# Head of the two mixture-of-experts stages: order of GpSimd's power, router-bias wait, position matmuls, and when the first weight slots are reloaded

## Chip, cores and metric

One core of one Trainium2 chip runs the whole program. The metric is device time of one execution in microseconds (us), and the figure compared is the median of the runs.

## What is computed

Two transformer blocks run one after the other on 256 tokens of width 1024, all in float32. Each is a mixer followed by a mixture of 32 experts (4 groups of 8). Only the expert part is touched by the change; cut to that:

```python
g_logits = x @ w_grp + b_grp;  g_idx = argmax(g_logits)        # 4 groups
e_logits = (x @ w_exp + b_exp)[group g_idx]                    # 8 experts of it
top_v, top_i = top_k(e_logits, 2)
gate = softmax(top_v) * softmax(g_logits)[g_idx]
for e in range(32):                                            # w1, w3: 1024x512, w2: 512x1024
    out += weight_e * ((silu(x_e @ w1[e]) * (x_e @ w3[e])) @ w2[e])
h = rmsnorm(h + out)
```

An expert's three matrices are 2,048 KB each, 6.29 MB together, so the weights of 32 experts are 201 MB in each of the two expert stages.

## The kernel before

**Stages.** `mixer1`, `moe` (first experts, "stage 1"), `mixer2`, `moe` again (second experts, "stage 2"). Between stages there is a barrier of all engines. Stage 1 starts at 192.2 us of the profiled execution and stage 2 at 1215.1 us.

**Weight sets.** SBUF holds two sets of three slots (w1, w3, w2) in `weight_ring`, and in stage 2 a third set, `e_third`. Expert `i` uses set `i % SETS`; SETS is 2 in stage 1 and 3 in stage 2. Experts 0 and 1 are loaded while the mixer before still runs (in stage 1 two matrices of expert 1 are loaded at the stage's start). The other loads are issued by the SyncE queue (SP), in one written order: for expert `i` it waits until expert `i - SETS` has finished its up projection (`s_up`), issues w1 and w3 (L1253, L1254, both by the helper's line L152), waits for that expert's down projection (`s_down`), and issues w2. An instruction on SP that waits holds up all that are queued behind it. `load_last` already loads the last two experts in halves.

**Head of a stage.** SP issues the router's weights (L1242, L1243: many short pieces), the router's biases (L1244, L1245), then in stage 1 the loads of the context part, and in stage 2 four pieces of `gate_m` (L1262), `final_row` (L1267) and the third set (expert 2). GpSimd (POOL) prepares `rw` and `halves`, then five small tables (L1310 to L1314), and then computes the inverse root with an ALU power (L1317) of the row statistics that VectorE (DVE) makes (L1517). With it ACT and DVE scale the rows (L1452, L1519), TensorE (PE) transposes them (L1329) and multiplies them by the router's weights (L1337; it waits for all four router loads, `s_router` 64). DVE adds the biases (L1546 to L1550) and picks the experts in a long chain of small instructions up to `both` (L1573). Five matmuls (L1355 to L1359) give each token its position in its expert (`ps` bank 4, columns 0 to 63) and each expert's total (columns 64 to 95). From the positions DVE makes `Gt` (L1580, L1582), PE gathers the rows of expert 0 (L1363), DVE transposes them (`xT`), and expert 0's up projection (L1398) begins.

**An expert on PE.** Up projection: 8 steps of k by 4 column blocks, 64 matmul records. Then the gather of the next expert, the combine of the one before (L1371) and the down projection (L1423). Expert 0 has the residual (L1346) in place of the combine, and a transposition of table rows (L1429). In stage 1, 18 groups of a projection of the context rows (L989, L991) are interleaved with experts 1 to 27, at fixed steps.

Of the kernel before, what the change touches and what calls it, by code (L numbers as in the profile page):

```python
# [5 lines left out]
ALU = mybir.AluOpType  # L6
# [9 lines left out]
TT = T // P  # L16
KD = D // P
# [13 lines left out]
NE, NG, EPG = 32, 4, 8  # L31
# [1109 lines left out]
def moe(c, t, w, last):  # L1141

    nc, ps, h = c.nc, c.ps, c.h
    with phase(nc, w["tag"]) as (st, sb, sem):
# [65 lines left out]
        s_router, s_frow, s_gm = sem("router_in"), sem("final_row_in"), sem("gate_in")  # L1210
# [30 lines left out]
        def _(sp):  # L1241
            sp.dma_start(rw[:, :, NE:RW], t[w["ew"]][0].rearrange("(k p) e -> p k e", p=P)).then_inc(s_router, 16)  # L1242
            sp.dma_start(rw[:, :, 0:NG], t[w["gw"]][0].rearrange("(k p) e -> p k e", p=P)).then_inc(s_router, 16)  # L1243
            sp.dma_start(rb[:, 0:NG], row_view(t[w["gb"]], 0, NG)).then_inc(s_router, 16)  # L1244
            sp.dma_start(rb[:, NG:NR], row_view(t[w["eb"]], 0, NE)).then_inc(s_router, 16)  # L1245
# [3 lines left out]
            def load_expert(u, e, done):  # L1249

                if done is not None:
                    sp.wait_ge(s_up, done)
                load_one(c, sp, sems, u, 0, W, e, third)  # L1253
                load_one(c, sp, sems, u, 1, W, e, third)  # L1254
                if done is not None:
                    sp.wait_ge(s_down, done)
                load_one(c, sp, sems, u, 2, W, e, third)

            if mod is not None:
                for m in range(4):  # L1260
                    at = 5 * D + m * 256
                    sp.dma_start(gate_m[32 * m:32 * m + 32, :], row_view(mod, at, at + 256, 32)).then_inc(s_gm, 16)  # L1262
# [5 lines left out]
            for i in range(2, STATIC):  # L1268
                load_expert(i % SETS, bass.ds(i, 1), i - SETS + 1 if i >= SETS else None)
                if x is not None:  # L1270
                    x.sp_step(sp, i)
            def load_last(u, e, done):
# [33 lines left out]
        def _(pool):  # L1306
            link = lambda ins: c.pch(pool, ins)
            pool.memset(rw[:, :, NG:NE], 0.0).then_inc(s_pad, 1)  # L1308
            pool.tensor_tensor(halves, c.ident[:, 0:RW], c.ident[:, RW:P], ALU.add).then_inc(s_pad, 1)  # L1309
            link(pool.iota(ie[:], [[1, NE]], base=0, channel_multiplier=0, allow_small_or_imprecise_dtypes=True))  # L1310
# [5 lines left out]
            pool.wait_ge(s_stat, 1)  # L1316
            pool.tensor_tensor(stat[:, 1, 0:TT], stat[:, 0, 0:TT], c.neg_half[:, 0:TT], ALU.pow).then_inc(s_rstd, 1)  # L1317
# [6 lines left out]
        def _(pe):  # L1324
# [6 lines left out]
            pe.wait_ge(s_router, 64)  # L1331
# [23 lines left out]
            pe.matmul(ps[:, 4, 0:NE], tri[:], both[:, 0, :], start=True, stop=True)  # L1355
            pe.matmul(ps[:, 4, NE:2 * NE], c.ones[:], both[:, 0, :], start=True, stop=False)
            pe.matmul(ps[:, 4, NE:2 * NE], tri[:], both[:, 1, :], start=False, stop=True)
            pe.matmul(ps[:, 4, 2 * NE:3 * NE], c.ones[:], both[:, 0, :], start=True, stop=False)
            pe.matmul(ps[:, 4, 2 * NE:3 * NE], c.ones[:], both[:, 1, :], start=False, stop=True).then_inc(s_pos, 1)  # L1359
# [18 lines left out]
            def expert(i, q, u):  # L1378
# [7 lines left out]
                for k in range(KD):  # L1386
                    if known and k == 0:
                        pe.wait_ge(s_w1[u], 16 * q + 16)
                        pe.wait_ge(s_w3[u], 16 * q + 16)
                    elif not known and k % 4 == 0:  # L1390
                        if k == 0:
                            pe.wait_ge(s_w1[u], 16 * q + (16 * TURNS + 16))
                            pe.wait_ge(s_w3[u], 16 * q + (16 * TURNS + 16))
                        else:
                            pe.wait_ge(s_half[2 * u], 16 * q + 16)
                            pe.wait_ge(s_half[2 * u + 1], 16 * q + 16)
                    for j in range(4):
                        mm = pe.matmul(ps[32 * j:32 * j + 32, 4, 0:256].rearrange("p (w f) -> p w f", w=2),  # L1398
                                       xT[:, k, :], w13[:, :, k, j * P:(j + 1) * P],
                                       start=(k == 0), stop=(k == KD - 1))  # L1400
                mm.then_inc(s_up, 1)
# [111 lines left out]
        def _(dve):  # L1513
# [17 lines left out]
            dve.wait_ge(s_router, 64)  # L1531
# [52 lines left out]
            link(dve.tensor_scalar(nblk[:], ps[:, 4, 2 * NE:3 * NE], float(SLOTS - 1), float(SLOTS), ALU.add, ALU.max))  # L1584
# [1000 lines left out]
```

## Time and profile before

| | us |
|---|---|
| median of 3 runs | 1696.2 (1696.05 to 1697.95) |
| the profiled execution: its time | 1696.79 |
| the profiled execution: its span | 1695.0 |
| PE busy | 1400.5 (83%) |
| DVE busy | 647.6 (38%) |
| ACT busy | 245.8 (15%) |
| POOL busy | 58.0 (3%) |
| DMA moved | 528.51 MB, mean 312 GB/s |

The span is what the trace shows; 1.8 us of the time lie around it. Busy shares are means over stages with different limits, so each stage is read by itself, from windows and the timeline.

### The profile page before, as it was taken

To read this page: it belongs to the slowest core of one execution; us is meant where nothing else is said; L and a number is where in the kernel's file an instruction comes from. 1 tells how busy PE (TensorE), PEld (TensorE's weight loads), DVE (VectorE), ACT (ScalarE), POOL (GpSimd) and SP (SyncE) were. 2 spreads that over 40 slices of the span, in tenths; PEclk is the share of its full clock that TensorE was granted. 3 is DMA by queue.
4 is the path that set the end of the run, shared out by engine and by line. 5 is a ranking of instruction groups with operands and counts; after the bars stand their busy time and mean duration, and the time that the engine had idled before them with its cause. 6 is when DMAs were issued, how large, how long until landed. Compare 5 with 4: busy or idle time off the path is not lost. (4 is left out here: it accounts for less than half of the span.)

```text
span 1695.0 us, 27911 instructions
## 1 busy us (share of the span) xinstructions
PE 1400.5 (83%) x12075; PEld 917.9 (54%) x12075; DVE 647.6 (38%) x1786; ACT 245.8 (15%) x502; POOL 58.0 (3%) x88
## 2 busy tenths in 40 slices
PE   7999798998779888769999999998787666666664
PEld 6556455665456555448865845887344333333332
DVE  3624347322233333321487732433264223333324
ACT  2321313100011111022222212211100000000000
POOL 1300100000000000020000100000000000000000
PEclk9999989999899888979999999999888777887878
DMA  9879488999999999974433242422889999999996
GB/s 338 240 271 372 152 338 348 421 415 422 415 417 414 421 415 420 423 262 149 150 112 112 82 156 85 149 100 77 332 369 427 427 426 426 428 426 426 428 424 255
DMA packets 110090, 528.51 MB, mean 312 GB/s; under 512 B 16680, under 2 KB 35312, under 8 KB 84368
## 3 DMA queue, kind: packets, MB, share of 16 engines
q1 hardware_dynamic: 105600, 522.70, 76.9%
q0 software_dynamic: 1936, 3.92, 1.0%
q8 instruction: 96, 1.57, 0.4%
q10 hardware_dynamic: 2432, 0.10, 0.1%
q14 instruction: 26, 0.21, 0.0%
HBM read 525.64 MB, written 1.06 MB: 311 GB/s over the span
## 5 line engine op out<-in xcount | busy, mean ns | idle before, releaser
L1398 PE MATMUL ps<-weight_ring,e_xT 128*32 128x256 f32 x3456 | 257.9, 463 | 164.1 <-DMA weight_ring<-in_w_up_dram 96.2
L1398 PEld LDWEIGHTS ps<-weight_ring,e_xT 128*32 128x32 f32 x3456 | 140.6, 132 | 277.4 <-issue 233.4
L1658 DVE TENSOR_TENSOR e_g<-e_act_g,ps 128x128 f32<-128x128 f32 x64 | 24.9, 389 | 274.0 <-ACT e_act_g L1481 272.9
L1481 ACT ACTIVATE e_act_g<-ps 128x128 f32<-128x128 f32 x64 | 17.8, 278 | 626.8 <-PE ps L1398 626.8
L1423 PE MATMUL ps<-weight_ring,e_gT 128*32 128x256 f32 x1728 | 104.4, 382 | 4.8 <-DVE e_gT L1662 1.5
L1656 DVE TENSOR_TENSOR e_act_g<-e_act_g,ps 128x128 f32<-128x128 f32 x32 | 9.2, 287 | 229.6 <-ACT e_act_g L1481 229.4
L1398 PE MATMUL ps<-e_third,e_xT 128*32 128x256 f32 x640 | 55.7, 524 | 46.3 <-DMA e_third<-in_w_up_dram 46.3
L989 PE MATMUL ps<-e_nT,e_ctx_w 128*128 128x256 f32 x320 | 76.2, 399 | 4.3 <-DVE e_ctx_gcols L1090 2.3
L1423 PEld LDWEIGHTS ps<-weight_ring,e_gT 128*32 128x32 f32 x1728 | 52.1, 109 | 49.7 <-issue 20.2
L1371 PE MATMUL ps<-e_y,e_GwT 32*128 32x256 f32 x1024 | 73.7, 402 | 2.1 <-DVE e_y L1690 1.5
L1363 PE MATMUL ps<-e_n,e_Gt 128*32 128x256 f32 x1056 | 72.8, 393 | 2.0 <-DVE e_Gt L1582 1.9
L989 PEld LDWEIGHTS ps<-e_nT,e_ctx_w 128*128 128x128 f32 x320 | 63.1, 200 | 17.0 <-issue 5.0
L1398 PEld LDWEIGHTS ps<-e_third,e_xT 128*32 128x32 f32 x640 | 30.1, 149 | 71.7 <-issue 67.3
L1371 PEld LDWEIGHTS ps<-e_y,e_GwT 32*128 32x128 f32 x1024 | 46.6, 185 | 30.5 <-issue 26.0
L991 PE MATMUL ps<-e_ctx_w,e_nT 128*128 128x256 f32 x256 | 59.5, 386 | 0.0
L2045 PE MATMUL ps<-weight_ring,m_nTp 128*128 128x512 f32 x128 | 57.2, 608 | 0.0
L1963 PE MATMUL ps<-weight_ring,m_nT 128*128 128x512 f32 x128 | 56.2, 592 | 0.0
L2089 PE MATMUL ps<-m_nT,weight_ring 128*128 128x256 f32 x256 | 56.2, 379 | 0.0
L1952 PE MATMUL ps<-m_nT,weight_ring 128*128 128x256 f32 x256 | 55.4, 379 | 0.0
L991 PEld LDWEIGHTS ps<-e_ctx_w,e_nT 128*128 128x128 f32 x256 | 47.3, 190 | 11.1 <-issue 5.3
L2089 PEld LDWEIGHTS ps<-m_nT,weight_ring 128*128 128x128 f32 x256 | 48.6, 190 | 6.6
L1952 PEld LDWEIGHTS ps<-m_nT,weight_ring 128*128 128x128 f32 x256 | 48.6, 190 | 6.6
(520 smaller groups left out, 1913.0 us busy)
## 6 DMA issues: line engine op xcount, KB each, us to landing
weight_ring<-in_expert_w_dram SPq DMA_DIRECT2D x92, 2048.0 KB, 19.6
weight_ring<-in_w_in_dram SPq DMA_DIRECT2D x26, 2048.0 KB, 8.4
weight_ring<-in_w_down_dram SPq DMA_DIRECT2D x22, 2048.0 KB, 39.3
weight_ring<-in_w_gate_dram SPq DMA_DIRECT2D x20, 2048.0 KB, 33.2
weight_ring<-in_w_up_dram SPq DMA_DIRECT2D x20, 2048.0 KB, 37.8
weight_ring<-in_w_ada_dram SPq DMA_DIRECT2D x12, 2048.0 KB, 9.0
e_third<-in_w_gate_dram SPq DMA_DIRECT2D x10, 2048.0 KB, 33.2
e_third<-in_w_up_dram SPq DMA_DIRECT2D x10, 2048.0 KB, 37.7
```

What stands on the lines that cost most here:

```text
L989: mm = pe.matmul(o, w[:, k, j * P:(j + 1) * P], nT[:, k, :], start=(k == 0), stop=(k == KD - 1))
L991: mm = pe.matmul(o, nT[:, k, j * P:(j + 1) * P], w[:, k, :], start=(k == 0), stop=False)
L1363: mm = pe.matmul(ps[32 * j:32 * j + 32, 5, 0:256], Gt[:, tt, :], n[:, tt, j * 256:(j + 1) * 256], start=(tt == 0), stop=(tt == TT - 1))
L1371: mm = pe.matmul(ps[:, m, tt * 256:(tt + 1) * 256], GwT[r, tt * P:(tt + 1) * P], y[r, :], start=False, stop=False, skip_group_check=True)
L1398: mm = pe.matmul(ps[32 * j:32 * j + 32, 4, 0:256].rearrange("p (w f) -> p w f", w=2), xT[:, k, :], w13[:, :, k, j * P:(j + 1) * P], start= ...
L1423: mm = pe.matmul(ps[32 * m:32 * m + 32, 5, 0:256], gT[:, j, :], w2[:, j, m * 256:(m + 1) * 256], start=(j == 0), stop=(j == KF - 1))
L1481: act.activation(act_g[:], ps[:, 4, 0:P], gated).then_inc(s_silu, 1)
L1658: dve.tensor_tensor(g[:], spread(act_g[:]), spread(ps[:, 4, P:2 * P]), ALU.mult).then_inc(s_g, 1)
L1952: mm = pe.matmul(ps[:, 4 + j % 4, 0:T], w[:, k, (j % 4) * P:(j % 4 + 1) * P], nT[:, k, :], start=(k == 0), stop=(k == KD - 1))
L1963: mm = pe.matmul(ps[:, 6 + j % 2, :], nT[:, k, tile * P:(tile + 1) * P], w[:, k, :], start=(k == 0), stop=(k == KD - 1))
L2045: mm = pe.matmul(ps[:, j % 4, :], nTp[:, k, tile * P:(tile + 1) * P], w[:, k, :], start=(k == 0), stop=(k == KD - 1))
L2089: mm = pe.matmul(ps[:, 2 + f % 2, 0:T], w[:, k, j * P:(j + 1) * P], rhs[:, k, :], start=(k == 0), stop=(k == KD - 1))
```

## The change

- POOL's power comes directly after the two preparations; then POOL issues the two bias loads itself, on its own queue (semaphore `s_rb`); the five small tables come after them.
- PE waits for the two router weight loads only (`s_router` 32); DVE waits for the biases (`s_rb` 32) ahead of the copy at L1546.
- The positions come from two matmuls (the first now 64 columns wide); the totals follow in two more, in bank 6, with a semaphore of their own (`s_tot`).
- Set 0's first reload (expert SETS) is issued in halves: the first halves of w1 and w3 when expert 0's up projection is half done (`s_uph`), the second halves when it is done.
- In stage 2 the third set is loaded ahead of `gate_m` and `final_row`.

```diff
+            if done == 1:                                    # in load_expert
+                for half in range(2):
+                    sp.wait_ge((s_uph, s_up)[half], 1)
+                    cs = slice(half * KD * FF // 2, (half + 1) * KD * FF // 2)
+                    for which in range(2):
+                        sp.dma_start(c.ring[:, which, cs].rearrange("p (o n) -> p o n", o=1),
+                                     W[which][0, e].rearrange("o (p k) f -> p o (k f)", k=KD)[:, :, cs]).then_inc((s_first, sems)[half][which], 16)
...
-            sp.dma_start(rb[:, 0:NG], row_view(t[w["gb"]], 0, NG)).then_inc(s_router, 16)
-            sp.dma_start(rb[:, NG:NR], row_view(t[w["eb"]], 0, NE)).then_inc(s_router, 16)
...
+            for i in range(2, SETS):
+                load_expert(i, bass.ds(i, 1), None)
             if mod is not None:
                 for m in range(4):
...
-            for i in range(2, STATIC):
-                load_expert(i % SETS, bass.ds(i, 1), i - SETS + 1 if i >= SETS else None)
+            for i in range(SETS, STATIC):
+                load_expert(i % SETS, bass.ds(i, 1), i - SETS + 1)
...
             pool.tensor_tensor(halves, c.ident[:, 0:RW], c.ident[:, RW:P], ALU.add).then_inc(s_pad, 1)
+            pool.wait_ge(s_stat, 1)
+            pool.tensor_tensor(stat[:, 1, 0:TT], stat[:, 0, 0:TT], c.neg_half[:, 0:TT], ALU.pow).then_inc(s_rstd, 1)
+            pool.dma_start(rb[:, 0:NG], row_view(t[w["gb"]], 0, NG)).then_inc(s_rb, 16)
+            pool.dma_start(rb[:, NG:NR], row_view(t[w["eb"]], 0, NE)).then_inc(s_rb, 16)
...
-            pool.wait_ge(s_stat, 1)
-            pool.tensor_tensor(stat[:, 1, 0:TT], stat[:, 0, 0:TT], c.neg_half[:, 0:TT], ALU.pow).then_inc(s_rstd, 1)
...
-            pe.wait_ge(s_router, 64)
+            pe.wait_ge(s_router, 32)
...
-            pe.matmul(ps[:, 4, 0:NE], tri[:], both[:, 0, :], start=True, stop=True)
-            pe.matmul(ps[:, 4, NE:2 * NE], c.ones[:], both[:, 0, :], start=True, stop=False)
-            pe.matmul(ps[:, 4, NE:2 * NE], tri[:], both[:, 1, :], start=False, stop=True)
-            pe.matmul(ps[:, 4, 2 * NE:3 * NE], c.ones[:], both[:, 0, :], start=True, stop=False)
-            pe.matmul(ps[:, 4, 2 * NE:3 * NE], c.ones[:], both[:, 1, :], start=False, stop=True).then_inc(s_pos, 1)
+            pe.matmul(ps[:, 4, 0:2 * NE], tri[:], both[:].rearrange("p t e -> p (t e)"), start=True, stop=False, skip_group_check=True)
+            pe.matmul(ps[:, 4, NE:2 * NE], c.ones[:], both[:, 0, :], start=False, stop=True, skip_group_check=True).then_inc(s_pos, 1)
+            pe.matmul(ps[:, 6, 0:NE], c.ones[:], both[:, 0, :], start=True, stop=False, skip_group_check=True)
+            pe.matmul(ps[:, 6, 0:NE], c.ones[:], both[:, 1, :], start=False, stop=True, skip_group_check=True).then_inc(s_tot, 1)
...
+                        if i == SETS:
+                            pe.wait_ge(s_first[0], 16)
+                            pe.wait_ge(s_first[1], 16)
...
+                    if known and i == 0 and k == KD // 2 - 1:
+                        mm.then_inc(s_uph, 1)
...
-            dve.wait_ge(s_router, 64)
+            dve.wait_ge(s_rb, 32)
...
-            link(dve.tensor_scalar(nblk[:], ps[:, 4, 2 * NE:3 * NE], float(SLOTS - 1), float(SLOTS), ALU.add, ALU.max))
+            dve.wait_ge(s_tot, 1)
+            link(dve.tensor_scalar(nblk[:], ps[:, 6, 0:NE], float(SLOTS - 1), float(SLOTS), ALU.add, ALU.max))
```

## Rows read from the trace of the kernel before

**Rows 1.** The page, part 2: GB/s moved in each of 40 slices of 42.4 us.

```profile
GB/s 338 240 271 372 152 338 348 421 415 422 415 417 414 421 415 420 423 262 149 150 112 112 82 156 85 149 100 77 332 369 427 427 426 426 428 426 426 428 424 255
```

**Rows 2.** Windows in stage 1: stretch, its us, busy by engine, PEclk, DMA share, GB/s.

```profile
218.00:220.00 2.00, 2.00 (x33) 0.85 (x25) 1.74 (x10) 0.00 (x0) 0.00 (x0) 0.82 0.89 143
...
250.00:254.00 4.00, 4.00 (x25) 3.16 (x28) 0.00 (x0) 0.77 (x2) 0.00 (x0) 1.00 0.32 131
...
282.00:286.00 4.00, 4.00 (x35) 3.01 (x37) 0.23 (x1) 0.77 (x2) 0.00 (x0) 1.00 0.37 160
```

**Rows 3.** Timeline of stage 1: start us, us, engine, line, instruction, [idle before <- releaser].

```profile
193.53 0.17 DVE L1517 TENSOR_SCALAR e_stat<-e_stat 128x2 f32<-128x2 f32 x1
...
194.81 0.70 POOL L1317 TENSOR_TENSOR e_stat<-e_stat,neg_half 128x2 f32<-128x2 f32 x1
...
198.02 19.60 SPq L859 DMA_DIRECT2D e_ctx_lbl<-in_hg_lb_logits_dram  x4
...
209.88 0.39 PE L1358 MATMUL ps<-e_both,ones 128*128 128x32 f32 x2
...
210.10 0.39 PE L1359 MATMUL ps<-e_both,ones 128*128 128x32 f32 x2
...
214.05 5.93 PE L1398 MATMUL ps<-weight_ring,e_xT 128*32 128x256 f32 x64 [1.08 <-DVE e_xT L1539]
...
253.59 3.66 PE L1398 MATMUL ps<-weight_ring,e_xT 128*32 128x256 f32 x64
...
285.08 1.93 PE L1423 MATMUL ps<-weight_ring,e_gT 128*32 128x256 f32 x32
```

**Rows 4.** Windows at the head of stage 2.

```profile
1224.00:1226.00 2.00, 2.00 (x14) 1.18 (x12) 0.41 (x1) 0.88 (x1) 0.00 (x0) 0.59 0.91 266
...
1242.00:1244.00 2.00, 2.00 (x36) 1.08 (x32) 1.79 (x12) 0.00 (x0) 0.00 (x0) 0.83 0.03 8
1244.00:1246.00 2.00, 2.00 (x19) 0.83 (x12) 1.79 (x10) 0.28 (x1) 0.00 (x0) 1.00 0.48 98
1246.00:1248.00 2.00, 2.00 (x6) 0.76 (x4) 0.30 (x1) 0.00 (x0) 0.00 (x0) 1.00 0.69 246
```

**Rows 5.** Timeline at the head of stage 2.

```profile
1216.23 4.08 SPq L1244 DMA_DIRECT2D e_rb<-in_b_group_dram  x1
...
1216.46 0.17 DVE L1517 TENSOR_SCALAR e_stat<-e_stat 128x2 f32<-128x2 f32 x1
...
1217.74 0.72 POOL L1317 TENSOR_TENSOR e_stat<-e_stat,neg_half 128x2 f32<-128x2 f32 x1
...
1218.50 0.75 DVE L1519 TENSOR_SCALAR e_n<-residual,e_stat 128x1024 f32<-128x1024 f32 x1 [1.87 <-POOL e_stat L1317]
...
1223.53 2.97 PE L1337 MATMUL ps<-e_nT,e_rw 128*64 128x256 f32 x16 [0.15 <-DMA e_rb<-in_b_router_dram]
...
1226.62 0.42 DVE L1546 COPY e_sq<-ps 128x256 f32<-128x256 f32 x1 [2.21 <-PE ps L1337]
...
1234.07 0.61 PE L1358 MATMUL ps<-e_both,ones 128*128 128x32 f32 x2
...
1234.49 0.61 PE L1359 MATMUL ps<-e_both,ones 128*128 128x32 f32 x2
...
1239.53 5.20 PE L1398 MATMUL ps<-weight_ring,e_xT 128*32 128x256 f32 x64 [1.56 <-DVE e_xT L1543]
...
1244.80 0.33 SPq L152 DMA_DIRECT2D weight_ring<-in_w_gate_dram  x1
...
1257.55 0.33 SPq L152 DMA_DIRECT2D weight_ring<-in_w_gate_dram  x1
```

**Rows 6.** Timeline: one load issued by POOL.

```profile
753.08 0.95 POOL L118 DMA_DIRECT2D expert_gain<-in_norm_g_dram  x1
```

**Rows 7.** View of line L1880: POOL's 8 loads of 256 KB, issue to landing.

```profile
DMA to landing us min/median/max: 3.7/6.2/7.6
```

**Rows 8.** Window in stage 2 while 1,024 KB halves of an expert flow.

```profile
1654.00:1658.00 4.00, 2.79 (x48) 1.39 (x40) 2.12 (x7) 0.00 (x0) 0.00 (x0) 1.00 0.99 416
```

More of the change, by code:

```diff
@@ L1208, in moe @@
         x = context(c, t, sb, sem, nT, sq, wide) if "context" in w else None
-        s_router, s_frow, s_gm = sem("router_in"), sem("final_row_in"), sem("gate_in")
+        s_router, s_rb, s_frow, s_gm = sem("router_in"), sem("router_bias_in"), sem("final_row_in"), sem("gate_in")
+        s_first, s_uph, s_tot = [sem(f"first_half_in{j}") for j in range(2)], sem("half_up_done"), sem("totals_done")
         s_sq, s_stat, s_rstd, s_n = sem("squares"), sem("stat"), sem("rstd"), sem("normed")
@@ L1249, in load_expert @@
             def load_expert(u, e, done):
[L1251 to L1254, printed above, removed]
+                if done == 1:
[5 more added lines that the diff above has]
+                                         W[which][0, e].rearrange("o (p k) f -> p o (k f)", k=KD)[:, :, cs]).then_inc((s_first, sems)[half][which], 16)
+                else:
+                    if done is not None:
+                        sp.wait_ge(s_up, done)
+                    load_one(c, sp, sems, u, 0, W, e, third)
+                    load_one(c, sp, sems, u, 1, W, e, third)
                 if done is not None:
```

## The prediction

> **What bounds the kernel now.** I read the page's slices first. In both expert stages the bytes moved stand near 425 GB/s for hundreds of microseconds (from 297 us on in stage 1, from 1271 us on in stage 2) [rows 1]. An expert is 6.29 MB, so at 425 GB/s it takes 14.8 us, and a stage's length is nearly its bytes over that rate. A stage therefore gets shorter only where the DMA engines stand idle while weights remain to be loaded, or ahead of that. I looked for those holes in windows of 2 and 4 us, and in the timeline for what ends each.
>
> Stage 2 has one hole: 8 GB/s moved in 1242 to 1244 [rows 4]. The third set is in, and nothing else may be loaded until set 0 is free. SP issues expert 3 at 1244.80, when expert 0's up projection (1239.53, 5.20 us) is done [rows 5]. In 1244 to 1248 only 0.69 MB moved in place of 1.70 MB [rows 4]; the missing 1.01 MB are 2.4 us of full rate, so the flow counts as restarted at 1246.4, 1.6 us after the issue. From there it does not stop. Everything from the stage's start to 1246.4 is therefore on the path, and it is a chain of small steps on DVE, POOL and PE.
>
> Stage 1 has two later holes, 131 GB/s in 250 to 254 and 160 GB/s in 282 to 286 [rows 2]. PE sets them, not the loads: expert 2's up projection starts at 253.59 behind context work with no wait for a load, and the second hole ends after expert 3's down projection (285.08, 1.93 us), which frees its slot [rows 3]. So up to 287 us stage 1 is a chain on PE, ACT and DVE that begins with the same head as stage 2; after that it is bytes.
>
> **Power first on POOL.** It could run when POOL is done with the two preparations and DVE with L1517. The latter ends at 193.70 and 1216.63, the power starts at 194.81 and 1217.74 [rows 3, 5]. With 0.1 us for the semaphore it starts at 193.8 and 1216.7: 1.0 us off each stage's head. The tables now come behind it and behind two bias issues of about 0.95 us each [rows 6]; the tables themselves are the 1.0 us by which the power was late, so they are done near 1220.5, and DVE first reads them behind L1546 (1226.62 [rows 5]). Cost nothing; without that cover each microsecond would count in full.
>
> **Bias later, from POOL.** In stage 2 PE lost only 0.15 us to the bias before L1337 [rows 5], but with the power 1.0 us earlier the bias would have eaten that gain, so the new wait is what lets it through. DVE's new wait sits in front of the copy, 1226.62 before [rows 5] and 1225.6 after; everything DVE does up to expert 0 is queued behind it. POOL issues the second bias load near 1218.4; with 3.7 to 7.6 us to landing [rows 7] it lands between 1222.1 and 1226.0. Those eight loads were 256 KB each, the biases are 4 and 32 numbers for each of 128 partitions, 2 and 16 KB, so I take the lower half and charge 0, with 0.4 us as the upper bound in stage 2 (the same sum in stage 1 gives up to 0.9 us). Taking two issues from SP moves its later loads forward by about a microsecond; nothing waits for those.
>
> The Trainium skill, "SBUF — State Buffer", section "SBUF: two separate sides", warns that a DMA issued by GpSimd has its descriptors written by GpSimd, which is locked out of the shared port while DVE runs a two-port instruction. No run here shows it. By that rule DVE's L1519 (0.75 us [rows 5]), released by the power at the moment when POOL turns to the bias loads, would delay them by up to 0.75 us; the late edge of 1226.0 would become 1226.7 and the sum at worst 1.1 us smaller in stage 2, at the middle of the landing times nothing.
>
> **Shorter positions.** Three of five matmuls leave the chain. Start to start they are 0.22 us apart in stage 1 and 0.42 us in stage 2, at granted clocks of 1.0 and 0.5 [rows 3, 5]. The 64-column one I price like the others, since weight loading of 128 columns is common to both; the upper bound is one step more. So 3 x 0.22 = 0.66 us and 3 x 0.42 = 1.27 us, lower bounds 0.44 and 0.85. The two totals matmuls run while DVE makes `Gt` and are over before the gather can begin; DVE's chain for the block counts has idle time behind it before the gathered rows come. Cost nothing.
>
> **Third set first.** The set is all in well before set 0 frees, so an earlier start alone gives nothing. What matters is the reverse, that SP must reach its wait for `s_uph` in time. The 4.08 us stall at L1244 [rows 5] looks like a queue full of the router's short pieces, and will now fall on the third set's first load, which still goes out by 1220.5. Then 6.3 MB plus 0.65 MB of gate and norm rows are in by about 1238.5, even if SP stays blocked until they are: two microseconds before `s_uph`. `gate_m` lands then too, before DVE wants it near 1243. Gain 0, loss 0; if SP came too late, the next part's gain would go.
>
> **Halves.** In stage 2 the clock rises inside this up projection: 0.83 over 1242 to 1244 is a rise at 1242.7 [rows 4]. Up to there, 3.15 us at half rate; the rest of the 64 records in 2.05 us at full rate. At twice the time per record that is 28 records and 36, so record 32 is over near 1242.9, 1.9 us before SP's issue. All at half rate it would be up to 3.4 us ahead. There is a cap. Set 1's reload is issued 12.8 us after set 0's (1257.55 less 1244.80 [rows 5]), and that distance is compute. The bytes of expert 3 last 14.8 us. So a lead of more than 14.8 - 12.8 = 2.0 us runs the engines dry before set 1 is free. Gain 1.9, at most 2.0, at least 0. In stage 1 it gives nothing: SP is held by the context loads at L859 until 217.6 [rows 3], and the bytes gained are only lost in the hole at 250, which PE ends.
>
> The skill's page "DMA: Bandwidth & Descriptors", section Bandwidth, speaks against cutting: 1 MB moves at 341 GB/s, 16 MB at 425. By that figure the four pieces would take 2.4 us longer (an estimate) and the halves would lose more than they bring. The row of this case disagrees, for pieces queued behind each other: 416 GB/s while such halves flow [rows 8]. I go by the row.
>
> **The sum.** Stage 1: 1.0 + 0.66 = 1.7 us. Stage 2: 1.0 + 1.27 + 1.9 = 4.2 us. Together 5.9 us off the profiled span's 1695.0 (its time 1696.79). That execution was 0.6 us above the median 1696.2, so I take the 5.9 us off the median: 1690.3. A result within 0.2%, 3.4 us, can't be told from no change by a measurement like this; so faster means below 1692.8.
>
> **Rivals.**
> A. As summed, with the clock rising as late after PE's start as before. 1690.3, own range 1688.5 to 1692. Chance 0.42.
> B. The clock's rise stays where it was in time, and work moved ahead of it runs at half rate. In stage 2 it rose at 1225.6 (0.59 over 1224 to 1226) and 1242.7 [rows 4]. A step moved forward across such an edge keeps half its gain. The router's matmuls keep 0.5 of 1.0; with the positions expert 0 starts 1.8 us earlier, and its end keeps about 1.0. With the cap of 2.0 on the lead, stage 2 gives 3.0. In stage 1 the rise is at 218.7 [rows 2]: 0.5 and 0.66 leave 1.2 at the start and 0.6 at the end. Together 3.6: 1692.6. For it: both up projections lie across such an edge. Against: the edge should not know when the kernel began. Chance 0.25. The Trainium skill, "TensorE: Matmul & The Clock Gate", Part 1, says the gate looks at activity in windows that run free of the kernel. By this rule B would hold in some executions and A in the mean; no run here shows it.
> C. The denser PE work raises the clock earlier, before expert 0's up projection in one or both stages. Its 5.20 and 5.93 us would go towards 3.66 us, the full-rate duration [rows 3, 5]: up to 1.5 and 2.3 us more. 1686.5 to 1688.5, middle 1687. Chance 0.12.
> D. One part gives nothing: stage 1's 1.7 us disappear in the context work (ACT, or a load of it), or SP is late for `s_uph` and the 1.9 us are missing. 1692.0 or 1692.2. Chance 0.12.
> E. Slower: POOL's bias load is served behind the third set's 6.3 MB instead of between. It would land near 1237.5, DVE's copy would start 12 us later than in A, and the reload of set 0 with it; stage 2 loses 12 less 4.2, stage 1's router biases are behind 6 MB likewise but only for some 2 us. 1690.3 + 12 + 2 = 1704. It decides when the stage 2 bias lands later than about 1231.5 (1225.6 plus the 5.9 us). For: SP's own loads wait for all before them. Against: POOL loads that ran beside streamed weights landed in at most 7.6 us [rows 7]. Chance 0.05. The remaining 0.04 is no effect at all.
>
> **Numbers.** The forecast is A, 1690.3. A, B, C and D lie between 1686.5 and 1692.6; with the noise of the median (up to 1.8 us) upwards, the range 1687 to 1694 leaves out E, no effect, and the low edge of C. Faster by over 3.4 us: A nearly whole, C, and over half of B and D, 0.72. Same: the rest of B and D and no effect, 0.22. Slower: E and some unseen wait, 0.06.
>
> **What would show it.** The power starting 0.1 us after L1517 in both stages; L1337 starting when the transposes end, without a bias wait; L1580 starting 0.6 us (clock 0.5) after the second position matmul begins; SP's first half issue about 2 us before `s_up`; a window like 1242 to 1244 moved to near 1238 and its restart 4 us earlier, with no new hole around 1257; the hole at 282 in stage 1 ending 1.7 us earlier. Wrong if L1546 is released by the bias, if a new hole follows expert 3's w2, or if the clock's edges stand still.

## The result and the profile after

The kernel with the change takes 1687.7 us (median of 5 runs, 1685.55 to 1688.24) beside 1696.2 us for the kernel before (5 runs, 1694.56 to 1699.08). The ratio is 0.9945, 95% interval 0.993 to 0.9959. The time fell by 8.5 us where the prediction's sum was 5.9.

The profiled execution took 1687.7 us, its span is 1686.0 (9.0 less than before). Stage 1 starts at 190.28 (before 192.19) and stage 2 at 1211.87 (before 1215.12). So 1.9 us came ahead of all changed code, 1.34 in stage 1 with the second mixer (1022.93 to 1021.59), and 5.75 in stage 2 (479.88 to 474.13). Times in the rows are absolute; to compare them with before, subtract the stage's start.

The head of stage 2 in the timeline of the kernel after (start, length, engine, line, instruction, idle before and its releaser), answering [rows 5]:

```profile
1212.98 4.16 SPq L152 DMA_DIRECT2D e_third<-in_w_gate_dram  x1
...
1213.22 0.17 DVE L1534 TENSOR_SCALAR e_stat<-e_stat 128x2 f32<-128x2 f32 x1
1213.47 0.72 POOL L1321 TENSOR_TENSOR e_stat<-e_stat,neg_half 128x2 f32<-128x2 f32 x1
...
1219.03 1.97 PE L1349 MATMUL ps<-e_nT,e_rw 128*64 128x256 f32 x16
...
1221.12 0.42 DVE L1563 COPY e_sq<-ps 128x256 f32<-128x256 f32 x1 [0.99 <-PE ps L1349]
...
1227.75 0.58 PE L1368 MATMUL ps<-e_both,ones 128*128 128x32 f32 x2
...
1228.44 0.23 DVE L1597 COPY e_pos<-ps 128x64 f32<-128x64 f32 x1 [0.89 <-PE ps L1368]
...
1232.76 5.32 PE L1413 MATMUL ps<-weight_ring,e_xT 128*32 128x256 f32 x64 [1.56 <-DVE e_xT L1560]
1236.42 0.35 SPq L1255 DMA_DIRECT2D weight_ring<-in_w_gate_dram  x1
...
1238.15 1.23 SPq L1255 DMA_DIRECT2D weight_ring<-in_w_gate_dram  x1
...
1250.90 0.33 SPq L152 DMA_DIRECT2D weight_ring<-in_w_gate_dram  x1
```

The power starts 0.08 us after its input. The router's matmuls follow the transposes without a wait and take 1.97 us where they took 2.97: that is not in the sum. The copy is released by PE, not by the bias. The first half is issued 1.7 us before the second; the next set is issued 12.75 us behind that second half. The stall of about 4 us that the bias issue had in [rows 5] is now the third set's.

The same stretch in windows of the kernel after (us, busy by engine, PEclk, DMA share, GB/s), answering [rows 4]:

```profile
1218.00:1220.00 2.00, 2.00 (x16) 1.37 (x16) 1.37 (x4) 1.70 (x3) 0.00 (x0) 0.72 0.60 222
...
1234.00:1236.00 2.00, 2.00 (x24) 0.99 (x20) 1.73 (x11) 0.00 (x0) 0.00 (x0) 0.50 0.64 213
1236.00:1238.00 2.00, 2.00 (x36) 0.85 (x28) 1.81 (x13) 0.00 (x0) 0.00 (x0) 0.96 0.40 68
1238.00:1240.00 2.00, 2.00 (x9) 1.04 (x6) 1.41 (x6) 0.28 (x1) 0.00 (x0) 1.00 0.86 311
1240.00:1242.00 2.00, 2.00 (x12) 0.68 (x15) 0.00 (x0) 0.00 (x0) 0.00 (x0) 1.00 1.04 438
```

The hole of 8 GB/s is one of 68. The clock rises at about 7.2 us after the stage's start (0.72 over 6.13 to 8.13) and again at about 24.3 (0.96 over 24.13 to 26.13). Before, [rows 4] put these rises at 10.5 and 27.6. Both rises came 3.3 us earlier. The up projection around the second one had moved by 3.52 us, the transposes ahead of the first by 1.04 (4.59 to 3.55 us into the stage).

Stage 1 in the timeline of the kernel after, answering [rows 3]:

```profile
191.87 0.71 POOL L1321 TENSOR_TENSOR e_stat<-e_stat,neg_half 128x2 f32<-128x2 f32 x1
...
194.27 21.44 SPq L859 DMA_DIRECT2D e_ctx_lbl<-in_hg_lb_logits_dram  x4
...
197.42 2.47 PE L1349 MATMUL ps<-e_nT,e_rw 128*64 128x256 f32 x16
...
200.34 0.42 DVE L1563 COPY e_sq<-ps 128x256 f32<-128x256 f32 x1 [1.94 <-DMA e_rb<-in_router_expert_b_dram]
...
207.24 0.23 DVE L1597 COPY e_pos<-ps 128x64 f32<-128x64 f32 x1 [0.46 <-PE ps L1368]
...
210.45 6.17 PE L1413 MATMUL ps<-weight_ring,e_xT 128*32 128x256 f32 x64 [1.10 <-DVE e_xT L1556]
...
281.72 1.93 PE L1440 MATMUL ps<-weight_ring,e_gT 128*32 128x256 f32 x32
```

Here the copy is released by the bias, 0.45 us after PE's end at 199.89, where a copy that PE releases follows by 0.12: about 0.3 us lost. The up projection starts 20.17 us after the stage's start (before 21.86). These 1.69 us are 0.79 at the copy, 0.67 at the positions and 0.23 in the gather, whose matmuls took 1.30 us where they took 1.55. Expert 3's down projection stands at 91.44 (before 92.89). SP is held by the context loads until 25.4 us, before and after.

The windows of the kernel after that answer [rows 2]; the holes are still there:

```profile
250.00:254.00 4.00, 4.00 (x70) 2.26 (x73) 2.77 (x6) 0.47 (x1) 0.00 (x0) 1.00 0.62 180
...
282.00:286.00 4.00, 4.00 (x80) 2.43 (x76) 3.34 (x8) 1.97 (x3) 0.00 (x0) 1.00 0.37 78
```

### The profile page after: what moved, and what is told of

It is laid out like the page before. It is cut to its first block and busy times, and to the rows that moved or that the text cites. A ratio compares the mean times of both kernels' runs of the same rounds, so it can differ in the third digit from the quotient of the medians.

```text
span 1686.0 us, 27909 instructions
## 1 busy us (share of the span) xinstructions
PE 1397.6 (83%) x12071; PEld 916.2 (54%) x12071; DVE 649.6 (39%) x1786; ACT 245.5 (15%) x502; POOL 60.7 (4%) x92
## 5 line engine op out<-in xcount | busy, mean ns | idle before, releaser
L989 PE MATMUL ps<-e_nT,e_ctx_w 128*128 128x256 f32 x320 | 76.4, 400 | 4.1 <-DVE e_ctx_gcols L1090 2.2
L989 PEld LDWEIGHTS ps<-e_nT,e_ctx_w 128*128 128x128 f32 x320 | 63.4, 201 | 16.7 <-issue 4.9
```

The lines of the kernel that those rows point to most:

```text
L989: mm = pe.matmul(o, w[:, k, j * P:(j + 1) * P], nT[:, k, :], start=(k == 0), stop=(k == KD - 1))
```

## Experiments

Each median stands beside runs of the kernel before on the same chip. Medians of one kernel scatter by 1 to 2 us, so they say whether a kernel won; the steps are read from the profiled executions, in which a stage 2 with an unchanged head repeats to 0.3 us. A run's profiled execution can stand anywhere among its times: late_power's was the fastest of 12, old_positions' the second slowest. "Length 1" is from stage 1's start to stage 2's, "length 2" from there to the end. "Experts 1" is from stage 1's start to the end of its last down projection; the rest of length 1 is the second mixer, whose code is the same everywhere.

| profiled execution | start of stage 1 | length 1 | experts 1 | up in stage 1: start, us | length 2 | up in stage 2: start, us | first reload, next set |
|---|---|---|---|---|---|---|---|
| before | 192.19 | 1022.93 | 539.2 | 21.86, 5.93 | 479.88 | 24.41, 5.20 | 29.68, 42.43 |
| before_again | 190.85 | 1022.77 | 539.0 | 21.86, 5.89 | 479.88 | 24.59, 5.15 | 29.81, 42.56 |
| after | 190.28 | 1021.59 | 538.1 | 20.17, 6.17 | 474.13 | 20.89, 5.32 | 24.55, 39.03 |
| again | 191.92 | 1019.04 | 535.5 | 20.29, 3.66 | 474.24 | 20.9, 5.3 | 24.58, 39.1 |
| stage_1_only | 191.83 | 1019.08 | 535.6 | 20.31, 3.66 | 480.19 | as before | as before |
| stage_2_only | 192.01 | 1022.68 | 539.0 | as before | 474.01 | 20.87, 5.26 | 24.47, 38.95 |
| no_halves | 190.30 | 1021.04 | 537.6 | 19.79, 6.30 | 476.86 | 21.10, 5.43 | 26.60, 39.35 |
| late_power | 190.38 | 1018.29 | 535.0 | 21.41, 5.54 | 477.23 | 23.02, 5.88 | 26.72, 41.72 |
| old_positions | 191.91 | 1022.6 | 539.1 | 20.79, 6.60 | 479.49 | 22.40, 6.49 | 26.10, 41.71 |
| bias_on_sp | 191.87 | 1025.4 | 539.4 | 22.32, 5.61 | 474.53 | 21.43, 5.36 | 25.13, 39.61 |
| third_late | 190.64 | 1019.08 | 535.5 | 20.33, 3.66 | 474.08 | 20.92, 5.34 | 24.61, as after |
| halves_only | 191.95 | 1025.41 | 539.4 | 21.85, 5.86 | 479.84 | 23.16, 6.20 | 26.87, 42.18 |

**The change again, and the kernel before again.** No edit.

> The changed kernel itself, run again beside the kernel before. Theory 1 (the heads alone are shorter; the 1.9 us by which the first mixer was shorter in the profile of after is chance): 7 to 7.5 us faster than before, so 1688.5 to 1689.5 where before is 1696.2, and in the profile the stages 1 start anywhere within 190 to 193 us, while stage 2 again lasts 474 us from its start to the end of the span (479.9 before). Rival (something outside the two heads became faster too): 9 us faster again, and stage 1 again starts near 190.3 us.

> The kernel before, as a run of its own, for a second profile and the spread. Theory 1: stage 2 again lasts 480 us and its granted clock again rises near 10.5 and 27.6 us after the stage's start (7.2 and 24.3 in after); stage 1's start differs from 192.2 us by up to 2 us, and its length (start of stage 1 to start of stage 2, 1022.9 us) by up to 2 us too. Rival (the 1.9 us ahead of stage 1 belong to the change): stage 1 starts at 192.2 again. Time the same as before.

Again: 1686.97, ratio 0.9956 (0.9939 to 0.9974). Before again: 1696.1, ratio 1.0001 (0.9992 to 1.001). The start of stage 1 moves between 190.3 and 194.2 over all executions with no bearing on the kernel, so the 1.9 us ahead of stage 1 were chance. Stage 1 shows two lengths with the change. In the timeline of again:

```profile
202.10 0.42 DVE L1563 COPY e_sq<-ps 128x256 f32<-128x256 f32 x1 [2.05 <-PE ps L1349]
...
212.21 3.66 PE L1413 MATMUL ps<-weight_ring,e_xT 128*32 128x256 f32 x64 [1.32 <-DVE e_xT L1556]
...
280.98 1.93 PE L1440 MATMUL ps<-weight_ring,e_gT 128*32 128x256 f32 x32
```

The up projection runs at full rate, expert 3's down projection is at 89.06 where it was at 91.44, and length 1 is 1019.04. With the change whole, or without the halves, up at 3.66 goes with 1019.0 to 1019.1 and up over 6 with 1021.0 to 1021.6; with the head of before it is 5.8 to 5.9 and 1022.7 to 1022.9 (halves_only is taken up below).

Late_power breaks this pattern: its up projection took 5.54 us, and its stage 1 is the shortest. What it saved lies behind expert 1, in 32 matmuls of the context projection (L989). First the timeline of after, then that of late_power:

```profile
240.29 10.13 PE L989 MATMUL ps<-e_nT,e_ctx_w 128*128 128x256 f32 x32 [1.15 <-ACT e_ctx_big L912]
```

```profile
241.02 7.17 PE L989 MATMUL ps<-e_nT,e_ctx_w 128*128 128x256 f32 x32 [1.15 <-ACT e_ctx_big L912]
```

They took 9.7 to 10.2 us in 13 of the 17 profiled executions, 8.7 and 8.9 in old_positions and hold_clock_both_and_residual, and 7.17 in late_power and quarters. In after the granted clock is at its lower level from 49.2 to 56.0 us into the stage, in late_power it is not. So the clock decides about some 3 us at a second place of stage 1. Which of the edits bear on that one is not shown.

**One stage alone.** The other stage runs the code of before.

```diff
-        moe(c, t, dict(EXPERTS_2, sets=3, gains=3 * GAIN, mod=mod[0:1, :], sems=c.s_e2, late=()), True)
+        moe_before(c, t, dict(EXPERTS_2, sets=3, gains=3 * GAIN, mod=mod[0:1, :], sems=c.s_e2, late=()), True)
```

That is stage_1_only; stage_2_only does it at the call for stage 1.

> The change in the first expert stage alone, the second as before. Theory 1: 1.3 to 3 us faster than before (head 1.7 us shorter, and, in some executions, expert 0's up projection 2.5 us shorter at the higher clock); stage 2 lasts 480 us. Rival (stage 1 gives the forecast's 1.7 us and no more, all the surplus is in stage 2): 1.5 us faster or less. Rival b: no gain.

> The change in the second expert stage alone. Theory 1: 5.8 us faster than before, stage 2 lasts 474.1 us. Rival (stage 2's length depends on where the clock's edges fall, and stage 1's change moves them): 476 us or more.

1689.9, ratio 0.9968 (0.9958 to 0.9977), and 1692.05, ratio 0.9979 (0.9969 to 0.9989). The two add up to the whole: 0.0032 + 0.0021 = 0.0053. But the medians divide it as 6.1 us for stage 1 and 3.9 for stage 2 (intervals of the ratios: 3.9 to 7.1 and 1.9 to 5.3), both off what was expected, and the profiles as 3.7 and 5.9; stage_1_only's profiled execution was the slowest of its nine. How the gain divides between the stages is thus shown for the profiled executions only.

**No halves, and halves alone.** In the first the reload of set 0 waits for the whole up projection; in the second only the halves are added to the kernel before.

```diff
-                if done == 1:
+                if False:
```

> The change without the halves (set 0's first reload is issued whole, when expert 0's up projection is done). Theory 1: only stage 2 becomes longer, by the lead of the first half's issue over the end of the up projection, 1.7 us in the profile of after; 1.7 us slower than the whole change, stage 2 lasts 475.8 us, stage 1 is unchanged. Rival a (the lead is used up at the next set, the cap of 2.0 us bites earlier): under 0.5 us slower. Rival b (stage 1 profits too): 3 us slower or more.

> The kernel before with the halves alone. Theory 1: the lead in stage 2 is 1.9 us and the cap 2.0, so stage 2 lasts 478.0 us (479.9 before) and stage 1 is unchanged at 1022.8; 1.9 us faster. Rival (the halves' gain is smaller than their lead, as the two stage lengths with and without them, 474.1 and 476.9, may owe 0.3 us to the clock): 1 us. Rival b: the cap bites and nothing is gained.

No halves: 1688.22, ratio 0.9953 (0.9936 to 0.997); length 2 is 2.7 us longer (1.7 was expected), with the first reload 2.05 later: 1.73 of lead, and an up projection that ends 0.34 later. The medians, 1.25 us apart, don't resolve it. Windows of no_halves:

```profile
1235.34:1237.34 2.00, 2.00 (x36) 1.07 (x32) 1.83 (x12) 0.00 (x0) 0.00 (x0) 0.82 0.07 20
1237.34:1239.34 2.00, 2.00 (x16) 0.87 (x9) 1.73 (x8) 0.28 (x1) 0.00 (x0) 1.00 0.44 90
```

Those are the two windows that moved 68 and 311 GB/s after. Halves alone: 1696.7, ratio 1.0005 (0.9992 to 1.0018), no gain, against what was expected. Its first reload is 2.8 us earlier than before's, as the up projection also started 1.25 earlier, but its next set only 0.25 (42.18 to 42.43): the lead of 2.57 us over its second half is above the cap of 2.0. 64 us into stage 2 it is 0.6 MB ahead (23.2 to 22.6 MB), 1.4 us. At the last expert 0.9 of it was left, and there the clock took that. First the timeline of before, then that of halves_only; the last expert's second half of w3 arrives 1675.57 - 1215.12 = 460.45 and 1676.90 - 1217.36 = 459.54 us into the stage:

```profile
1675.57 3.09 PE L1398 MATMUL ps<-weight_ring,e_xT 128*32 128x256 f32 x32 [2.96 <-DMA weight_ring<-in_w_up_dram]
```

```profile
1676.90 3.64 PE L1410 MATMUL ps<-weight_ring,e_xT 128*32 128x256 f32 x32 [2.85 <-DMA weight_ring<-in_w_up_dram]
```

So a lead of 1 us in bytes isn't yet 1 us at the end: the tail behind the last byte has a clock of its own. Length 1 was 2.5 us longer here with a head like before's. The experts were done at 539.4 and 539.2 us, and until 840 us into the stage both had moved the same bytes, so it came in the second mixer. Why is open.

**Late power, and old positions.** The first puts the tables back ahead of the power, the second puts the five matmuls back.

```diff
-            pool.wait_ge(s_stat, 1)
-            pool.tensor_tensor(stat[:, 1, 0:TT], ..., ALU.pow).then_inc(s_rstd, 1)
...
             pool.affine_select(...)                          # the last table
+            pool.wait_ge(s_stat, 1)
+            pool.tensor_tensor(stat[:, 1, 0:TT], ..., ALU.pow).then_inc(s_rstd, 1)
```

> The change with the power and POOL's two bias loads behind the five tables, as the power was before. Theory 1: each head 1.0 us longer, and 2.0 to 3.0 us slower in all than the whole change (stage 2's router matmuls fall back to the lower clock for one more microsecond, up to 1.0 us more). Rival (the power's 1.0 us is eaten by the waits for the bias from POOL, which come 1.0 us later here too): 0 to 1 us slower.

> The change with the five position matmuls of before. Theory 1: 0.7 us longer head in stage 1 and 1.3 us in stage 2 (spacing 0.22 and 0.42 us, three matmuls), together 2.0 us slower than the whole change. Rival (the clock's rise stands still, so that an earlier start of expert 0 gives back only half): 1.0 us slower.

Late power: 1690.58, ratio 0.9973 (0.9961 to 0.9985). Timeline of late_power:

```profile
1211.28 0.72 POOL L1327 TENSOR_TENSOR e_stat<-e_stat,neg_half 128x2 f32<-128x2 f32 x1
...
1216.84 3.08 PE L1349 MATMUL ps<-e_nT,e_rw 128*64 128x256 f32 x16
...
1231.69 5.88 PE L1413 MATMUL ps<-weight_ring,e_xT 128*32 128x256 f32 x64 [1.56 <-DVE e_xT L1560]
```

The power is 1.02 us later, the router's matmuls take 3.08 in place of 1.97, and the up projection starts 2.13 later: in stage 2 the early power is worth 1.0 by itself and 1.1 through the clock, and length 2 is 3.1 us longer without it. Windows of late_power, whose stage 2 starts at 1208.67:

```profile
1218.00:1220.00 2.00, 1.92 (x12) 0.83 (x8) 0.00 (x0) 0.42 (x1) 0.00 (x0) 0.70 0.96 393
1235.00:1237.00 2.00, 2.00 (x32) 0.98 (x28) 1.81 (x12) 0.00 (x0) 0.00 (x0) 0.69 0.40 61
```

They put the rises at 10.5 and 27.6 us into the stage, where they were in the kernel before. The up projection started 1.38 us earlier than before and ended 0.70 earlier (28.91 for 29.61): it kept half. Old positions: 1691.66, ratio 0.9976 (0.9965 to 0.9988). From the start of L1367 to `pos` it is 2.45 us in place of 1.17, so 1.28. Its up projection takes 6.49 and its halves lead by 2.8 us, more than the 2.0 allowed, and a dip follows where set 1 isn't free yet; 0.36 MB are missing in it, 0.9 us of full flow. Length 2 is 5.4 us longer than after's, where 1.3 was expected: 170 MB of the stage are moved 3.1 us later, and the other 2.3 come behind, at the last experts, and are not placed. Windows of old_positions (full flow is 425):

```profile
1253.00:1255.00 2.00, 2.00 (x44) 1.22 (x40) 1.89 (x5) 0.00 (x0) 0.00 (x0) 1.00 0.95 373
1255.00:1257.00 2.00, 1.89 (x40) 0.91 (x32) 1.47 (x6) 0.28 (x1) 0.00 (x0) 1.00 0.99 401
1257.00:1259.00 2.00, 2.00 (x36) 1.14 (x32) 1.82 (x6) 0.00 (x0) 0.00 (x0) 1.00 0.97 320
```

**Bias on SP, and third set late.** The first issues the two bias loads from SP behind the router's weights, still waited for by DVE; the second loads the third set behind `gate_m` and `final_row` again.

```diff
+            sp.dma_start(rb[:, 0:NG], row_view(t[w["gb"]], 0, NG)).then_inc(s_rb, 16)
+            sp.dma_start(rb[:, NG:NR], row_view(t[w["eb"]], 0, NE)).then_inc(s_rb, 16)
...
-            pool.dma_start(rb[:, 0:NG], row_view(t[w["gb"]], 0, NG)).then_inc(s_rb, 16)
-            pool.dma_start(rb[:, NG:NR], row_view(t[w["eb"]], 0, NE)).then_inc(s_rb, 16)
```

> The change with the two bias loads back on SP's queue, between the router's weights and the loads behind them; the waits stay as changed (PE two loads, DVE the biases). Theory 1: stage 1's copy behind the router matmuls no longer waits for the bias (0.3 us in the profile of after) and stage 2's did not wait; so 0 to 0.4 us faster than the whole change, stage 2 lasts 474 us. Rival (moving the issues off SP was worth something, through the third set's earlier start or the context loads): 1 us slower or more.

> The change with the third set's loads behind gate_m and final_row again. Theory 1: the third set's bytes then end about 1 us later, just as the first half's bytes could flow (24.6 us after the stage's start plus 1.6), so 0 to 0.5 us slower. Rival (third set first is what the halves need: without it their bytes queue behind the third set): stage 2 is 1.0 to 1.9 us longer.

Bias on SP: 1690.99, ratio 0.997 (0.996 to 0.9981). Timeline of bias_on_sp:

```profile
200.17 1.06 ACT L880 ACTIVATE e_wide<-e_ctx_big 128x1024 f32<-128x1024 f32 x1 [1.07 <-DMA e_ctx_big<-in_ctx_dram]
...
205.85 3.68 PE L894 MATMUL ps<-ident,e_ctx_big 128*128 128x128 f32 x16 [2.61 <-ACT e_ctx_big L887]
...
207.98 0.22 DVE L1590 TENSOR_TENSOR e_both<-e_hot 128x64 f32<-128x64 f32 x1
...
209.32 0.53 PE L1367 MATMUL ps<-e_both,e_tri 128*128 128x64 f32 x2
```

The context rows land later, their transposes (L894) reach PE 1.1 us later (13.99 for 12.92) and at half rate, and the positions, ready at 208.2, wait behind them until 209.3. Up starts 22.32 us into the stage, 2.15 later than after. So POOL's issue pays by what it takes off SP in stage 1, an edit costed at nothing. Of the 3.8 us in length 1, 1.3 are in the experts (539.4 to 538.1); the other 2.5 are in the second mixer, as in halves_only, and are no cost of this edit that is shown. Third set late: 1686.67, ratio 0.9951 (0.9936 to 0.9966), and length 2 is 474.08. That part gives nothing.

**Extra matmuls against the clock's fall.** All four kernels add matmuls of the identity by rows that are there, into a bank that nobody reads. warm_before_positions puts 5 of 512 columns ahead of the positions in both stages. warm_twice has 4 of 256 ahead of the transposes as well. hold_clock_stage_1 has fewer, in stage 1 alone, and hold_clock_both_and_residual in both, and it moves the residual of stage 2 (L1346 before) behind expert 1's up projection. The diff is that last one's.

```diff
+            def keep(count, n):
+                for _ in range(count):
+                    pe.matmul(ps[:, 7, 0:n], c.ident[:], h[:, 0, 0:n], start=True, stop=True)
+            if x is None: keep(4, 256)                        # ahead of the transposes; stage 2
...
+            keep(*((2, 256) if x is not None else (5, 512)))  # ahead of the positions: stage 1, else 2
...
+            keep(*((1, 256) if x is not None else (1, 128)))  # ahead of expert 0's gather
...
+            keep(2, 256)                                      # behind it
...
+                elif x is None and second:                    # behind expert 1's up
+                    residual()
```

> The change with five more 512-column matmuls on PE, into the unused bank 7, in its pause ahead of the position matmuls, in both stages; nothing reads them. Theory 1 (the change's gain beyond the sum is the clock: what PE did before a stretch decides its rate): the clock is 1.0 in the positions, the gather and expert 0's up projection; that one takes 3.66 us in place of 5.32, the gather 1.1 in place of 1.9, the positions 0.4 us less; stage 2 is 2.5 to 3 us shorter, 471.3 us, stage 1 0.5 to 2.5 us. Rival (the clock's edges stand still whatever PE does): stage 2 stays at 474 us.

> As e7, and four more 256-column matmuls ahead of the transposes at the head of each stage. Theory 1: the transposes (3.67 us) and the router's matmuls (1.97 to 2.5 us) run at the higher clock too, some 2 us less if the clock is up by then, 0 if these four matmuls are too short to raise it; so 0 to 2 us faster than e7. Rival: the added matmuls hold up the transposes, which start later than 3.55 us after the stage's start; slower than e7.

> The change with five matmuls of 256 columns on PE in stage 1 alone, into the unused bank 7, two ahead of the position matmuls, one behind the totals, two behind the gather, in pauses of about 1 us each; nothing reads them. Theory 1 (whether expert 0's up projection in stage 1 runs at 3.66 or 6.2 us is decided by what PE did just before): it takes 3.7 us, stage 1 lasts 1019.1 us, and the median is up to 1.3 us below the whole change's 1687.5. Rival (the fall comes whatever is in the pauses): up projection above 5 us in stage 1, length 1021 or more, and the added matmuls cost up to 0.5 us.

> As e14, and in stage 2 more such matmuls (four ahead of the transposes, five of 512 columns ahead of the positions, three around the gather) with the residual's matmuls moved behind expert 1's up projection, which lifts the cap of 2.0 us on the lead; the halves stay halves. Theory 1: transposes 2 us, expert 0's up projection 3.7 us, up projection done near 22.8 us after the stage's start in place of 26.2, first half issued near 21; the third set's bytes end at 24, so the flow has no hole any more, and stage 2 is 2 us shorter than 474.1. Rival (the clock falls again before the up projection, as in e8, but the residual's move alone lifts the cap): 1 us shorter. Rival b: no gain, as in e12.

warm_before_positions: 1690.2, ratio 0.9961 (0.9949 to 0.9973); warm_twice: 1688.81, 0.9963 (0.9948 to 0.9978). In stage 2 the up projections end 0.5 and 0.8 us earlier than after and length 2 is 473.89 in both, where 471.3 was expected: the positions and, in part, the gather ran at the higher level, but the clock fell at 17.4 us into the stage, and up took 5.73 and 6.19 us. In stage 1 the five matmuls are too many. Timeline of warm_before_positions:

```profile
210.35 0.22 DVE L1592 TENSOR_TENSOR e_both<-e_hot 128x64 f32<-128x64 f32 x1
210.43 4.46 PE L1366 MATMUL ps<-e_n,ident 128*128 128x512 f32 x10
214.72 0.33 PE L1369 MATMUL ps<-e_both,e_tri 128*128 128x64 f32 x2
```

There the context's transposes fill PE's pause up to about a microsecond, so the matmuls begin as the positions are wanted and push them back by some 4 us. hold_clock_stage_1: 1687.61, ratio 0.9952 (0.9934 to 0.9969); its up runs at 3.66 us and length 1 is 1019.24, at the good value of the table, but the median isn't below again's. hold_clock_both_and_residual: 1683.08 (6 runs, 1680.15 to 1686.21), ratio 0.9922 (0.9905 to 0.9938), 4.5 us below the former (bootstrap on the runs: 0.8 to 8.5). Timeline of hold_clock_both_and_residual, stage 2 (from 1211.78):

```profile
1215.33 2.32 PE L1347 MATMUL ps<-ident,e_n 128*128 128x128 f32 x16 [0.60 <-ACT e_n L1480]
1218.21 1.95 PE L1355 MATMUL ps<-e_nT,e_rw 128*64 128x256 f32 x16 [0.56 <-DMA e_rw<-in_w_group_dram]
...
1221.26 4.51 PE L1339 MATMUL ps<-residual,ident 128*128 128x512 f32 x10
1226.43 0.43 PE L1374 MATMUL ps<-e_both,e_tri 128*128 128x64 f32 x2 [0.67 <-DVE e_both L1601]
...
1230.85 3.66 PE L1422 MATMUL ps<-weight_ring,e_xT 128*32 128x256 f32 x64 [0.73 <-DVE e_xT L1571]
```

The transposes take 2.32 in place of 3.67, and the router's matmuls then wait for a router load. The matmuls against the fall end before the positions are wanted, and up takes 3.66 and ends 22.73 us into the stage (after 26.21). Length 2 is 470.92, 3.2 us less; 2.1 of them show in the bytes (170 MB at 402.3 us for 404.4). Its stage 1 had length 1021.48 with up at 3.66. In that execution the clock was low ahead of the positions: the same 2 extra matmuls took 1.92 us where hold_clock_stage_1 shows 1.03, and up started at 22.20 where there it was 20.90. What the clock and what the moved residual gave was not taken apart; quarters (below) has the residual moved too, without these matmuls, and its length 2 is 473.94.

**Quarters.** Set 0's reload in four parts from the middle of the up projection, with the same moved residual.

```diff
+                    for part_ in range(4):
+                        sp.wait_ge(*((s_uph, part_ + 1) if part_ < 3 else (s_up, 1)))
...
+                    if known and i == 0 and k in (1, 3, 5):
                         mm.then_inc(s_uph, 1)
```

> Two steps beyond the change: set 0's first reload in quarters (each pair of 512 KB pieces issued when a quarter of expert 0's up projection is done), and in stage 2 the residual's matmuls (3.7 us on PE) moved behind expert 1's up projection, so that set 1 is free 3.7 us earlier and the cap of 2.0 us on the lead rises. Theory 1 (bytes alone set stage 2 behind its head): the hole of after at 24 to 28 us closes, stage 2 is 1.5 to 2.2 us shorter than after's 474.1. Rival (the small pieces, or the later residual, cost as much): 474 us or more.

1686.51, ratio 0.9946 (0.9932 to 0.9959). The reload starts 1.7 us earlier (22.89) and the next set 3.2 earlier (35.84), yet length 2 is 473.94. Windows of quarters:

```profile
1236.66:1238.66 2.00, 1.62 (x32) 0.72 (x28) 1.70 (x10) 0.28 (x1) 0.00 (x0) 1.00 0.94 311
1238.66:1240.66 2.00, 1.38 (x29) 0.71 (x24) 1.88 (x5) 0.00 (x0) 0.00 (x0) 1.00 0.91 281
1240.66:1242.66 2.00, 2.00 (x31) 1.41 (x24) 0.80 (x5) 0.00 (x0) 0.00 (x0) 1.00 1.01 299
```

The engines are busy, but while the quarters are issued near 300 GB/s move, where the halves made 438. By 32 us into the stage both kernels have moved about 11.1 MB, and the lead is gone. The size of the pieces isn't shown to be the reason: the last quarters landed 37.9 us into the stage, and in the windows ahead of that the flow was near full again:

```profile
1242.66:1244.66 2.00, 2.00 (x27) 1.54 (x29) 0.78 (x2) 0.00 (x0) 0.00 (x0) 1.00 1.00 389
1244.66:1246.66 2.00, 2.00 (x44) 1.22 (x40) 0.52 (x1) 0.00 (x0) 0.00 (x0) 1.00 1.03 422
```

## Why the prediction was right and wrong

Right: the two holes, and that stage 2's chain up to the reload is the path. The parts by their own sizes: the power started 1.02 us earlier (1.0), the positions gave 1.28 in stage 2 and 0.67 in stage 1 (1.27 and 0.66). In stage 1 the start of up came 1.7 earlier (1.7), with some luck: the bias took about 0.3 and the clock gave 0.23 in the gather. The halves lead by 1.7 (1.9), and the cap of 2.0 on the lead shows in old_positions and halves_only. What the lead is worth came out as 2.4 in one pair (no_halves, less 0.34) and as nothing in the other (halves_only). The third set gave 0. That the halves fall behind SP's context loads in stage 1 held too (25.4 us).

Wrong is the step that fixed the clock: rival A's "with the clock rising as late after PE's start as before". PE's transposes began 4.59 us into stage 2 and the clock rose at 10.5, 5.9 us behind; in after they began at 3.55 and it rose at 7.2, 3.7 behind. This step mis-sized two terms of the sum.

1. Stage 2 was 4.2 and measured 5.75. The copy came 2.25 us earlier where 1.0 was counted: 1.02 power, 1.0 from the router's matmuls (2.97 to 1.97), which before had run their first 2.1 us at half clock, and 0.2 from the waits in front of them. Late_power has the copy at 11.38 and halves_only at 10.25 with the same power time, 2.61. The router's matmuls took 1.95 to 2.27 us in every stage 2 with an early power whose transposes were left alone, and 1.95, 2.88, 2.97, 3.08 and 3.08 in those with a late one, though PE began its work at the same time in all five of these. So the late head had the low clock mostly, not always. The first reload is 5.13 earlier: 3.52 from the start of up, -0.12 from its length, 1.73 from the lead. In bytes the gain is 4.9 (170 MB at 404.4 us for 409.3), so about 0.8 of the 5.75 came at the last experts and is not placed.

2. Stage 1 was 1.7 and measured, against before's 1022.93, 1.3 and 1.9 where up took over 6 us (after, no_halves), 3.2 in quarters (up 5.19, length 1019.72) and 3.8 to 3.9 where it ran at full rate (again, stage_1_only, third_late). From after to again it is rival C's mechanism: 2.51 us less in the up projection, 2.55 less in length 1. Its chance of 0.12 was much too low for stage 1. In quarters the up projection gave 1.0 against after and L989 3.0, of which some was lost again behind it; late_power, with 4.6, has 3.0 of them from L989 too. No part of the prediction costed that stretch.

The mean of the six values of stage 1 is 3.0, and 5.75 + 3.0 = 8.75 beside medians of 8.5 and 9.1. Six profiled executions of five kernels carry no more than that the size fits; the profiled execution of after has 1.9 us of chance ahead of stage 1 in it. Rival C's time, 1687, is the one that came, though in stage 2 by the router's matmuls and not by the up projection, which stayed at 5.32.

Rival B fell for the change whole: the rises came 3.3 us earlier. But late_power shows its mechanism, the rises where they were and half of the earlier start kept, and the fall between them stayed near 14.0 us into the stage in before, after and late_power alike. When a rise moves with the work and when it stands is not settled by these runs. The Trainium skill, "TensorE: Matmul & The Clock Gate", Part 1, has the gate follow PE's activity; the trace agrees in so far as hold_clock_both_and_residual shows 3.66 us where PE was kept busy.

The bias, costed at nothing, released the copy in stage 1 of after, which the prediction had named as a sign of being wrong. It took 6.8 us to land there and 4.1 in stage 2, where "the lower half" of 3.7 to 7.6 was assumed for both. The cost was 0.3 us in after and nothing in again, where PE's matmuls were the later. In quarters PE was done 1.23 us before the copy and the bias cost 1.1, above the bound of 0.9. In stage 2 a bias from POOL was never late. Rival D didn't come in either form, nor did E. Against "nothing waits for those", said of SP's later loads, bias_on_sp lost in stage 1 by delaying them.

The same size of error twice had one origin: half-rate stretches were seen in the rows and taken as given, though a microsecond at the head can decide whether a stretch of 3 or 5 us behind it runs at half or full rate.

## What to carry to other kernels

Cost a chain at the head of a stage with both clock levels for each PE group in it, and put the chance on the pair; where PE's groups of some microseconds stand near an edge, the clock can be worth as much as the edit. Matmuls that keep the clock up paid where PE had a pause that they fitted into with room to spare, up to the work that was to run fast (3.2 us of stage 2, together with the moved residual), and cost their length where it hadn't. Cutting the first reload in two gives at most what the distance to the next free set allows, and alone it gave nothing; cutting it in four gave nothing more.

## What the runs showed of the hardware

- While pieces of 512 KB were issued in sequence 281 to 311 GB/s moved, at a DMA share of 0.91 to 1.01; pieces of 1,024 KB moved 438 and 416 [rows 8]. The Trainium skill, "DMA: Bandwidth & Descriptors", section Bandwidth, says that small transfers reach less. This case agrees only in part, as the last 512 KB pieces were still landing at 389 and 422 GB/s.
- In stage 2 the issue behind the router's weights stalls SP by 4.1 us whatever it loads: 4.08 for a bias of 2 KB [rows 5], 4.16 for 2,048 KB. In bias_on_sp and halves_only two issues in a row shared the stall (2.1 and 2.8 us, 1.8 and 2.8); it ended 5.2 to 5.4 us into the stage in all of these. In stage 1 the issue at the same place took 0.57 us, before and after.
- Two loads of 2 and 16 KB issued by POOL took 6.5 and 6.8 us to land in stage 1 of after and 3.6 and 4.1 in stage 2.
- The same code in the same kernel (stage 1 of after and of again) ran its first up projection at 6.17 and 3.66 us, and the whole stage was 2.5 us shorter with the latter.
